# Adding the parts of u on DVE instead of POOL, and the parameter operations one block later

## What is computed

```python
u = rmsnorm(h, g_pre)
p = u @ w_in                      # 12 * 1024 + 8 columns
log_f = jax.nn.log_sigmoid(f_logit + b_forget)   # the 8 extra columns
o_fox, o_sb = attention with log_f, stick-breaking attention
o_ssm = s5_mixer(su, a_re, a_im, log_dt, ...) * silu(ssm_gate)
o_lru = rglru_mixer(lx, ..., lru_lambda) * silu(lru_gate)
return h + rmsnorm(concatenate([o_fox, o_sb, o_ssm, o_lru]) @ w_out, g_post)
```

## Time and profile before

| | us |
|---|---|
| median of 3 runs | 1529.48 (1528.81 to 1529.86) |
| the profiled execution | 1528.07 |
| its span, first to last instruction | 1526.1 |
| PE busy | 1511.2 (99%) |
| PEld busy | 1244.2 (82%) |
| DVE busy | 947.7 (62%) |
| ACT busy | 875.4 (57%) |
| POOL busy | 130.6 (9%) |
| mean granted TensorE clock | 0.999 of full speed |

### The profile page before, as it was taken

One profiled execution on the slowest core, in us unless ns is written; L12 is line 12 of the kernel. 1 busy time (PEld: TensorE's weight loads), 2 busy tenths in 40 slices (PEclk: granted clock), 3 DMA queues, 4 the chain that ended last, 5 costly groups with the idle time before them and its releaser, 6 DMA issues.

```text
span 1526.1 us, 21924 instructions
## 1 busy us (share of the span) xinstructions
PE 1511.2 (99%) x7086; PEld 1244.2 (82%) x7086; DVE 947.7 (62%) x1170; ACT 875.4 (57%) x1182; POOL 130.6 (9%) x164
## 2 busy tenths in 40 slices
PE   8899999999999999999999999999999999999998
PEld 7787888888888888888888888888888888888886
DVE  5663468898888995566554555455556544444445
ACT  6654476667766666666764544566666443444443
POOL 0510001221202210000001010000000000000000
PEclk9999999999999999999999999999999999999999
DMA  8465556655555655555666555565556866666675
GB/s 323 143 193 166 185 171 193 186 181 186 186 185 184 196 181 187 192 186 188 185 210 199 170 178 170 161 199 172 165 165 208 292 191 198 193 193 193 194 228 190
DMA packets 86704, 292.42 MB, mean 192 GB/s; under 512 B 9976, under 2 KB 13312, under 8 KB 86528
## 3 DMA queue, kind: packets, MB, share of 16 engines
q1 hardware_dynamic: 78480, 280.27, 57.6%
q10 hardware_dynamic: 8176, 11.54, 2.2%
HBM read 287.56 MB, written 4.20 MB: 191 GB/s over the span
## 4 chain that ended last, share of the span: by engine, by line
PE 97%; DMA 1%; DVE 1%; ACT 0%; SPq 0%; issue 0%; ACTq 0%
PE main L304 30%; PE main L306 30%; PE main L305 30%; PE main L345 1%; DMA w_raw<-in_wall 1%; PE main L491 1%; PE side L432 1%; PE main L443 1%; PE main L493 0%; PE side L524 0%; PE side L515 0%; PE side L479 0%; PE main L597 0%; PE main L596 0%; PE main L595 0%; DVE w_lo L1003 0%
## 5 line engine op out<-in xcount | busy, mean ns | idle before, releaser
L1003 DVE TENSOR_TENSOR w_lo<-w_raw,w_hi 128x1024 fp32r<-128x1024 f32 x518 | 640.8, 1241 | 544.9 <-ACT w_hi L627 544.3
L627 ACT ACTIVATE w_hi<-w_raw 128x1024 fp32r<-128x1024 f32 x518 | 544.9, 1057 | 535.0 <-PE main L306 509.6
L304 PE MATMUL main<-w_hi,acts 128*128 128x512 f32 x2024 | 797.3, 394 | 5.5 <-ACT cross L642 5.1
L306 PE MATMUL main<-w_hi,acts 128*128 128x512 f32 x2024 | 788.8, 390 | 0.0
L305 PE MATMUL main<-w_lo,acts 128*128 128x512 f32 x2024 | 788.4, 390 | 0.0
L304 PEld LDWEIGHTS main<-w_hi,acts 128*128 128x128 f32 x2024 | 380.4, 188 | 87.5 <-issue 9.2
L306 PEld LDWEIGHTS main<-w_hi,acts 128*128 128x128 f32 x2024 | 380.3, 188 | 80.4
L305 PEld LDWEIGHTS main<-w_lo,acts 128*128 128x128 f32 x2024 | 380.6, 188 | 77.4
L1561 POOL TENSOR_TENSOR scr<-scr 128x256 f32<-128x256 f32 x32 | 31.3, 978 | 409.3 <-ACT scr L712 409.3
L1253 DVE TENSOR_TENSOR_SCAN vals<-small,vals 128x256 f32<-128x256 f32 x64 | 42.5, 704 | 0.0
L642 ACT ACTIVATE cross<-main,small 128x512 f32<-128x512 f32 x40 | 27.5, 689 | 23.6 <-PE main L306 17.8
(11 more groups left out here) (278 smaller groups left out, 836.9 us busy)
## 6 DMA issues: line engine op xcount, KB each, us to landing
w_raw<-in_wall SPq DMA_DIRECT2D x511, 512.0 KB, 3.5
br<-in_x SPq DMA_DIRECT2D x16, 256.0 KB, 7.6
w_raw<-in_wglu SPq DMA_DIRECT2D x8, 512.0 KB, 3.9
out<-br SPq DMA_DIRECT2D x5, 512.0 KB, 2.8
br<-in_gpost ACTq DMA_DIRECT2D x8, 256.0 KB, 5.4
vals<-in_x ACTq DMA_DIRECT2D x8, 256.0 KB, 5.6
scr<-in_x ACTq DMA_DIRECT2D x8, 256.0 KB, 4.2
scr<-in_bt ACTq DMA_DIRECT2D x32, 32.0 KB, 2.1
```

Of the source, the lines that this page charges most:

```text
L304: pe.matmul(main[:, bank0 + a, :], u_h, wh, start=(k == 0), stop=False)
L306: mm = pe.matmul(main[:, bank0 + a, :], u_l, wh, start=False, stop=(k == NK - 1))
L627: act.activation(w_hi[:, c % RING, :], w_raw[:, c % RING, :], ACT.Copy).then_inc(hi_ready, 1)
L1003: dve.tensor_tensor(w_lo[:, c % RING, :], w_raw[:, c % RING, :], w_hi[:, c % RING, :].bitcast(F32), ALU.subtract).then_inc(lo_ready, 1)
```

## The change

DVE makes the 16 additions: one behind the low part of each chunk of the second block (`sum_parts`), after one wait for the last low part of `u`. POOL's 16 additions and its wait are gone. `PAR_BLOCK` becomes 2, so all parameter operations on DVE and ACT stand behind the same chunk numbers of the third block, beside the steps of the forget logits.

```diff
-        PAR_BLOCK = 1
+        PAR_BLOCK = 2
...
+            def sum_parts(k):
+
+                dve.tensor_tensor(u_sum[k // 16][:, k % 16:k % 16 + 2, :], acts[:, k:k + 2, 0:T].bitcast(F32),
+                                  acts[:, k:k + 2, T:2 * T].bitcast(F32), ALU.add).then_inc(u_ready, 1)
+
             def src_block(i):
                 for c in range(CH):
                     low(i, c + LEAD)
+                    if i == 1:
+                        if c == 0:
+                            dve.wait_ge(u_lo, NK)
+                        sum_parts(2 * c)
...
-            pool.wait_ge(u_lo, NK)
-            for k in range(0, NK, 2):
-                pool.tensor_tensor(u_sum[k // 16][:, k % 16:k % 16 + 2, :], acts[:, k:k + 2, 0:T].bitcast(F32),
-                                   acts[:, k:k + 2, T:2 * T].bitcast(F32), ALU.add).then_inc(u_ready, 1)
```

## The result

| | before | after |
|---|---|---|
| median of 6 runs, us | 1529.18 (1528.64 to 1529.86) | 1520.95 (1520.69 to 1521.84) |
| the profiled execution, its span | 1528.07, 1526.1 | 1521.2, 1519.5 |

The ratio is 0.9946 (95% interval 0.9934 to 0.9959): 8.2 us faster. The forecast was 1522.6 with a range from 1521.2 to 1525.0. The direction was right; the time lies 0.25 us under the range, and the gain was 1.3 us larger than my sum.

What follows compares the result with a forecast made beforehand. PE bounds the kernel, its one long wait being for the norm's root, held up by POOL. Gap 5.26 plus clock 1.64 make 6.9 us, other terms 0: 1529.5 - 6.9 = 1522.6 us, range 1521.2 to 1525.0.

Steps and rivals of the forecast that it cites:

- my sum: Gain for the whole kernel: 5.26 us from PE's gap plus 1.64 from the clock behind it, 6.9 us.
- What bounds, and the gap (5.26 us): PE, 99% busy, waits after the first block for the norm's root, slowed by POOL; removing POOL's additions gains 5.26 us.
- The clock behind the gap (1.64 us): Second block's first eight matmuls ran at half clock, 3.45 us against 1.81; full clock gains 1.64 us.
- From the profile to the median (1.4 us): The profiled execution lay 1.4 us under the median, so the forecast 1521.2 was shifted to 1522.6 us.
- DVE's additions at no cost: Second block: 16 additions of 0.70 us each fill 1.49 us of idleness behind each low part, cost 0.
- The parameter operations at no cost: Third block: DVE busy 16.9 of 19.0 us, falls behind by 1.3 us and recovers; cost 0, bounds 0 and 2.6.
- A: Rival: the root's five steps are slow for another reason that stays; 1529.5 us, chance 0.04.
- B: Rival: crowding in the third block makes PE wait once, costing 2.6 us; 1525.2 us, chance 0.05.
- C: Rival: DVE's additions bound the second block, slower than before; 1531.8 us at 2.33 us each, chance 0.03.
- D: Rival: each DVE instruction holds the engine longer than its row; 1536.6 us if twice, chance 0.01.
- C's formula: Second block: if DVE's addition costs x, PE waits 16 (x - 1.49) - 5.87 us.
- the ring: High parts may start when the chunk four before is used, so low parts are ready 5.87 us early.

Runs made afterwards that it cites:

- e3: The kernel before with only the parameter operations moved to the third block, POOL still adding: 1528.63 us, ratio 0.9999.
- e6: The kernel before with 84 small matmuls, results unread, on PE ahead of the second block's first chunk: 1526.89 us, ratio 0.9986.
- e2: The changed kernel with the parameter operations left in the second block, so only the additions move to DVE: 1521.66 us, ratio 0.9955.
- e7: The changed kernel with 24 memsets of 128x1024 on POOL from the last low part of u on: 1521.32 us in one run.
- e8: The changed kernel with each addition made four times by DVE: 1538.32 us in one run.
- e9: The changed kernel with the two identity matrices made first on POOL and PE's first wait for these alone: 1521.66 us, ratio 0.9952.
- e12: The same kernel as e2, only the additions moved to DVE, run again beside e11: 1521.92 us, ratio 0.9955.
- e11: The changed kernel unedited, run again on the same chip as e12: 1521.33 us, ratio 0.9952.
- e4: The kernel before with POOL's 16 additions waiting for the norm's root first: 1526.55 us, ratio 0.9986.

## Why the prediction was wrong, and what of it was right

- **What bounds, and the gap (5.26 us).** Right. DVE's steps, the copy at 58.73 (58.42 forecast, and 0.24 of the difference is the later end of the first block), no remaining gap, and the same gap in every profile of the kernel before. One reading was incomplete: PE's list had a second long wait, 3.9 us at the start, which neither kernel touches.
- **The clock behind the gap (1.64 us).** The mechanism was right, the term was mis-sized, and this is the step that failed. It was read from one execution and put into the sum as a fixed 1.64 us, but it varies from one execution to the next: 1.64, 1.87 and 2.8 us in three profiles of the same kernel, 1.91 in e3, and 2.2 to 2.35 on the average by e6. That is 0.4 to 0.7 us more.
- **From the profile to the median (1.4 us).** I shifted the sum by the distance of the profiled execution from the median, as if this distance belonged to both kernels. But part of it was the short slow stretch, which the change removes: it should have been in the gain and not in the shift. This is the same error seen from the other side, and it helped to put the range too high. Another 0.3 us of the 1.4 was the base: the median of three runs was 1529.48, that of six 1529.18. The range's low end allowed for scatter of the runs and for no term larger than the one read.
- **The rest.** 5.26 and 2.05 to 2.35 make 7.3 to 7.6. Another 0.2 us lies outside the span: a run's time less its span is 1.95 us in each kernel where POOL adds (before, e3 to e6) and 1.7 in those where it doesn't (the change, e2, e7, e8, e9, e12). I have no cause for it. The sum, 7.5 to 7.8, lies between the two comparisons of the same two kernels, 8.2 and 7.3. These differ by more than the 0.25 us by which the range was missed, and e11's median, 1521.33, would have been inside it.
- **DVE's additions at no cost.** Right: 0.69 us against 0.70, in a hole of 1.5. A low part and an addition took 1.74 us from start to start (64.13 to 65.87), against 1.93.
- **The parameter operations at no cost.** Right within what can be measured (e2, e3, e11, e12). What I didn't see is that they need the new place if POOL's additions are only delayed (e4).
- **The rivals.** A fell with e2 and e4; B, C and D with PE's list, which has only the wait at the start. C's formula gives 13.2 us for e8's DVE, and PE's two waits came to 14.5: it held for the ring but missed that PE asks for the last addition directly.

## What to carry to other kernels

When a busy engine waits once for a chain of tiny operations, look at how long each takes and what another engine does at that moment. Ask it of every small tensor_tensor and tensor_scalar of DVE beside POOL's reading (both took 1.2 us here instead of 0.16), and put POOL's long work where only long, covered operations meet it. Price a gap of PE with the slow clock behind it, and take that part from several executions or a kernel that fills the gap, never from one profile. When a profile lies off the median, ask which term made it so before the distance is added to both kernels.

## What was not expected of the hardware

- The slow stretch behind the same 5.3 us gap cost 1.64 to 2.8 us from one execution to the next, at half the granted clock (0.50).
- Filling a gap of PE with matmuls whose results nobody reads is worth 2.35 us here, though PE waits as long as before.
- A low part of 128x1024 that meets POOL's reading is lengthened by up to 1.1 us (from 1.22 to 2.35, e4), a 128x2 step by as much: from 0.16 to 1.2 us. So many small steps lose far more than one long one.
